# Attention A of a two-layer decoder: mask by an identity product, values and queries ahead

## The reference

```python
q_lat, c_kv, q_idx, k_idx, w_idx = split(h @ w_in)      # 16 heads of 128 latents; one c_kv of 128
c_kv = rms_norm(c_kv, latent_g)
score = sum_j w_idx[j] * relu(q_idx[j] @ k_idx.T)       # the indexer, 8 heads of 64
idx = top_k(where(causal, score, -inf), 128)            # 128 keys a query
logits = q_lat @ c_kv[idx].T * 128**-0.5 + rel_bias[bucket(t - idx)]
p = softmax(where(idx <= t, logits, -inf))
o = p @ c_kv[idx]                                       # latent, 128 wide, for each head
out = (o @ w_uv[head]) @ w_out                          # 128 -> 64 a head, 16 heads -> 1024
```

## Time and profile before

| | |
|---|---|
| runs | 1254.78, 1253.8, 1253.1 us; median 1253.8 |
| profiled execution, span from first to last instruction | 1252.3 us |
| PE busy | 1192.8 us (95%) |
| DVE busy | 638.1 us (51%) |
| ACT busy | 467.7 us (37%) |
| POOL busy | 573.3 us (46%) |
| query projection behind the indexer | 107 to 167 us |
| heads of attention A | 168 to 305 us |

### The profile page before, as it was taken

How to read it: one execution, slowest core, us unless ns; L and a number is a source line. 1 busy time by engine, 2 the same in 40 slices (tenths; PEclk the granted TensorE clock), 3 DMA queues, 4 the chain that set the end, 5 groups by cost and what they waited for, 6 DMA issues and landing times.

```text
span 1252.3 us, 16936 instructions
## 1 busy us (share of the span) xinstructions
PE 1192.8 (95%) x5580; PEld 976.2 (78%) x5580; DVE 638.1 (51%) x1095; ACT 467.7 (37%) x872; POOL 573.3 (46%) x336
## 2 busy tenths in 40 slices
PE   5999988889999999999999999899999999999996
PEld 4757877668888888888888778788888888888885
DVE  5458989995554444442222368846644444431111
ACT  4243146765333223333222367643333322232222
POOL 4333476663444444443444464304444444444441
PEclk9999999999999999999999999899999999999998
DMA  5712321102333333333333342303233333323331
GB/s 161 248 36 68 120 60 39 39 29 77 94 101 100 100 96 87 88 88 92 93 92 103 101 111 59 68 1 101 79 91 100 100 100 100 90 70 93 92 92 67
DMA packets 178709, 110.37 MB, mean 88 GB/s; under 512 B 7425, under 2 KB 173372, under 8 KB 178668
## 3 DMA queue, kind: packets, MB, share of 16 engines
q1 hardware_dynamic: 178224, 108.69, 30.4%
q10 hardware_dynamic: 444, 1.16, 0.3%
HBM read 107.70 MB, written 6.33 MB: 91 GB/s over the span
## 4 chain that ended last, share of the span: by engine, by line
PE 85%; DVE 8%; issue 3%; DMA 1%; ACT 1%; POOL 0%; DVEq 0%; ACTq 0%; SPq 0%
PE ps L608 28%; PE ps L610 27%; PE ps L609 27%; DVE prob L1547 1%; PE ps L781 1%; DVE raw L1547 1%; DMA q_all<-in_x 1%; DVE b_prob L1742 1%; DVE prob L1569 1%; DVE ss L1437 1%; DVE xs_lo L1380 1%; DVE raw L1569 1%; DVE xs_lo L1424 1%; PE ps L938 1%; DMA raw<-in_b_w_in 0%
## 5 line engine op out<-in xcount | busy, mean ns | idle before, releaser
L480 POOL TENSOR_TENSOR w_lo<-raw,w_hi 128x1024 fp32r<-128x1024 f32 (+1 forms) x200 | 462.8, 2335 | 560.2 <-ACT w_hi L1033 560.1
L608 PE MATMUL ps<-xs_hi,w_hi 128*128 128x512 f32 x960 | 380.2, 396 | 5.5 <-DVE x L1420 3.7
L609 PE MATMUL ps<-xs_lo,w_hi 128*128 128x512 f32 x960 | 374.3, 390 | 0.0
L610 PE MATMUL ps<-xs_hi,w_lo 128*128 128x512 f32 x960 | 374.2, 390 | 0.0
L1033 ACT CAST w_hi<-raw 128x1024 fp32r<-128x1024 f32 (+1 forms) x200 | 183.0, 964 | 470.2 <-PE ps L610 457.8
L608 PEld LDWEIGHTS ps<-xs_hi,w_hi 128*128 128x128 f32 x960 | 180.6, 188 | 50.9 <-issue 6.1
L610 PEld LDWEIGHTS ps<-xs_hi,w_lo 128*128 128x128 f32 x960 | 180.5, 188 | 37.9
L609 PEld LDWEIGHTS ps<-xs_lo,w_hi 128*128 128x128 f32 x960 | 180.7, 188 | 37.3 <-issue 1.2
L608 PE MATMUL ps<-act_hi,w_hi 128*128 128x512 f32 x352 | 139.2, 396 | 0.0
L610 PE MATMUL ps<-act_hi,w_lo 128*128 128x512 f32 x352 | 138.0, 392 | 0.0
L609 PE MATMUL ps<-act_lo,w_hi 128*128 128x512 f32 x352 | 136.6, 388 | 0.0
(11 more groups left out here) (191 smaller groups left out, 1568.6 us busy)
## 6 DMA issues: line engine op xcount, KB each, us to landing
raw<-in_ffn_w_gate_up SPq DMA_DIRECT2D x88, 512.0 KB, 4.9
raw<-in_ffn_w_down SPq DMA_DIRECT2D x32, 384.0 KB, 3.6
raw<-in_a_w_in SPq DMA_DIRECT2D x21, 512.0 KB, 4.6
raw<-in_ffn_w_down SPq DMA_DIRECT2D x32, 320.0 KB, 4.0
raw<-in_b_w_in SPq DMA_DIRECT2D x10, 512.0 KB, 5.1
bias_toep<-bias_row SPq DMA_DIRECT2D x1, 4096.0 KB, 19.2
toep<-bias_toep SPq DMA_DIRECT2D x16, 256.0 KB, 2.6
raw<-in_a_w_out SPq DMA_DIRECT2D x8, 512.0 KB, 4.0
```

The costliest lines, as they stand in the source:

```text
L480: nc.gpsimd.tensor_tensor(pieces(w_lo, n)[half], pieces(raw, n)[half], pieces(w_hi, n)[half].bitcast(F32), ALU.subtract)\
L608: nc.tensor.matmul(dst, wh, xh, start=start, stop=False, **kw)
L609: nc.tensor.matmul(dst, wh, xl, start=False, stop=False, **kw)
L610: return nc.tensor.matmul(dst, wl, xh, start=False, stop=stop, **kw)
```

## The change

- **Mask and bias.** POOL's sum bm is gone. PE adds the mask (written by DVE as an fp32r tile) with a product by an identity, ahead of the logits of blocks 1 to 3, and lowest adds toep straight. The causal bound of the diagonal comes in the bias table: a 33rd row of 1e30 for columns from 512 on.
- **Values ahead.** w_uv of all heads comes in one transfer; values = c @ w_uv are made once, in eight triples (values, steps 0 and 1), split by ACT and DVE into the free weight slots. The product of probabilities with them (weigh, now in step k for head k-3, two PSUM banks in turn) gives 64 columns of a head at once; the second product, o_hi, o_lo and c_hi, c_lo go.
- **Queries ahead.** q_scale writes one of two small tiles; ACT and POOL split each query during the projection into q_hi and q_lo of all 16 heads. q_scale(h) waits for q_part(h-2). Tile 15 joins the projection.
- **Slabs.** w_out's first slab is split by ACT in steps 12 and 13, its second after the last weigh; all loops over heads are written out.
- **Scaling** by 1/row sum stays on DVE, with invert at the head of the step.

The diff, cut to its core:

```diff
@@ sync @@
             slab(2, 0, wide(a_w_in[0], A_QI + 256))
+            sp.dma_start(uv_raw[:, :, :], a_w_uv[0].rearrange("h r c -> r h c")).then_inc(uv_full, 16)
             sp.wait_ge(row_out, 16)
...
-                    sp.wait_ge(bias_done, 4 * (h - 1))
+                    sp.wait_ge(neg_done, 4 * (h - 1))
@@ gpsimd @@
-            split_lo(S_A2 + 2)
-            split_lo(S_A2 + 3)
-            q_part(0, 0)
-            q_part(1, 1)
...
-                        nc.gpsimd.tensor_tensor(bm[:, OFF[i]:OFF[i] + n], toep[:, par, T - n:T], mask, ALU.add)\
-                            .then_inc(bias_done, 1)
...
+            def q_part(h):
+                if h == 0:
+                    pool.wait_ge(row_out, 16)
+                pool.wait_ge(qh_done, h + 1)
+                nc.gpsimd.tensor_tensor(q_lo[:, h, :], q_new[h % 2], q_hi[:, h, :].bitcast(F32),
+                                        ALU.subtract).then_inc(ql_done, 1)
+            for i in range(6):
+                q_part(2 * i)
+                q_part(2 * i + 1)
+                split_lo(S_A2 + 2 + i)
+                if i == 1:
+                    pool.wait_ge(uvh_done, 1)
+                    nc.gpsimd.tensor_tensor(uv_lo[:, :, :], uv_raw[:, :, :], uv_hi[:, :, :].bitcast(F32),
+                                            ALU.subtract).then_inc(uvl_done, 1)
+            for h in range(12, H):
+                q_part(h)
+            for n in range(S_AO, S_F0 + 2):
                 split_lo(n)
@@ tensor @@
-            pe.wait_ge(cn_done, 1)
-            for s in range(NB):
-                last = nc.tensor.transpose(ps[:, 7, s * P:(s + 1) * P], c_nrm[:, s * P:(s + 1) * P], ident)
-            last.then_inc(c_tr, 1)
...
             for v in range(3):
                 q_tile(v, 2)
+            tile(ps[:, 3, :], S_A2 + 7, 0, P, 256, xh, xl)
...
+            def values(j):
...
+                mm3(ps[:, 4 + s, :], cT_hi[:, s * P:(s + 1) * P], cT_lo[:, s * P:(s + 1) * P],
+                    uv_hi[:, h0:h0 + 8, :], uv_lo[:, h0:h0 + 8, :], True, True).then_inc(av_mm, 1)
+            def logits(k):
...
+                        if i:
+                            nc.tensor.matmul(ps[:, b, c0:c0 + n], ident_r[:, :], mask[:, OFF[i] - P:OFF[i] - P + n],
+                                             start=True, stop=False)
+                        last = mm3(ps[:, b, c0:c0 + n], q_hi[:, k, i * P:(i + 1) * P],
+                                   q_lo[:, k, i * P:(i + 1) * P], cT_hi[:, 0:n], cT_lo[:, 0:n], i == 0, True)
...
+            for k in range(H + 3):
+                if 2 <= k < H + 2:
+                    turn(k - 2)
+                if k >= 3:
+                    weigh(k - 3)
+                if k < H:
+                    logits(k)
+                if k < 2:
+                    for j in range(4 * k, 4 * k + 4):
+                        values(j)
...
+                if k >= H:
+                    out_first(S_AO, oT_hi, oT_lo, oTl_done, range(2 * (k - H), 2 * (k - H) + 2), 2)
@@ scalar @@
                 if i == 2:
                     split_after(S_A2)
+                    q_head(0)
+            q_head(1)
...
+            nc.scalar.copy(uv_hi[:, :, :], uv_raw[:, :, :]).then_inc(uvh_done, 1)
...
+            q_head(2)
+            for i in range(5):
+                split_after(S_A2 + 1 + i)
+                q_head(2 * i + 3)
+                q_head(2 * i + 4)
...
+            for k in range(H + 3):
+                if 2 <= k < H + 2:
+                    turned_hi(k - 2)
+                if k >= 4:
+                    heads_hi(k - 4)
+                if k < H:
+                    exponents(k)
+                if k < 2:
+                    for j in range(4 * k, 4 * k + 4):
+                        value_hi(j)
+                if k in (12, 13):
+                    split_late(S_AO, k - 12, 8)
+            heads_hi(H - 1)
+            for half in range(2):
+                split_late(S_AO + 1, half, H)
@@ vector @@
-            def q_scale(h, bank):
+            def q_scale(h, bank, par):
                 dve.wait_ge(unit_done, U_A2 + 1 + h)
-                nc.vector.scalar_tensor_tensor(q_all[:, h, :], ps[:, bank, :], -float(R) ** -0.5, rstd[:, :],
+                if not (isinstance(h, int) and h < 2):
+                    dve.wait_ge(ql_done, h - 1)
+                nc.vector.scalar_tensor_tensor(q_new[par], ps[:, bank, :], -float(R) ** -0.5, rstd[:, :],
                                                ALU.mult, ALU.mult).then_inc(qa_done, 1)
...
-            dve.wait_ge(c_h, 1)
-            lo_part(c_lo[:, :, :].rearrange("p a b -> p (a b)"), ps[:, 7, :],
-                    c_hi[:, :, :].rearrange("p a b -> p (a b)").bitcast(F32), c_l)
             for r in range(4):
                 topk_round(r)
-            q_scale(3, 3)
+            q_scale(3, 3, 1)
...
+            for k in range(H + 3):
+                if 1 <= k <= H:
+                    invert(k - 1)
+                if k >= 4:
+                    heads_lo(k - 4)
+                if 2 <= k < H + 2:
+                    turned_lo(k - 2)
+                if k < H:
+                    lowest(k)
+                if 1 <= k <= H:
+                    normalise(k - 1)
+                if k < 2:
+                    for j in range(4 * k, 4 * k + 4):
+                        value_lo(j)
+            heads_lo(H - 1)
```

More of the change, by code:

```diff
@@ new lines, in weigh @@
+            def weigh(h):
+                pe.wait_ge(ptl_done, 3 * h + 3)
+                if h >= 2:
+                    pe.wait_ge(oTl_done, h - 1)
+                for s in range(NB):
+                    c0 = (0, 4, 7, 9)[s] * P
+                    n = (NB - s) * P
+                    last = mm3(ps[:, 6 + h % 2, s * P:T], v_pair(w_hi, h, s), v_pair(w_lo, h, s),
+                               pt_hi[:, h % 2, c0:c0 + n], pt_lo[:, h % 2, c0:c0 + n], s == 0, s == NB - 1)
+                last.then_inc(o_done, 1)
@@ L849, in feed_forward @@
+            out_first(S_AO, oT_hi, oT_lo, oTl_done, range(6, DM), 2)
             def feed_forward(layer, e, s_gu, s_d):
@@ L1103, in _, with q_head @@
             split_after(2)
+            def q_head(h):
+                act.wait_ge(qa_done, h + 3)
+                nc.scalar.copy(q_hi[:, h, :], q_new[h % 2]).then_inc(qh_done, 1)
             act.wait_ge(craw_done, 1)
@@ new lines, in split_late, with turned_hi @@
+            def split_late(n, half, heads):
+                act.wait_ge(raw_full[n % 2], 32 * (n // 2 + 1))
+                act.wait_ge(o_done, heads)
+                nc.scalar.copy(pieces(w_hi, n)[half], pieces(raw, n)[half]).then_inc(hi_done, 1)
+            def turned_hi(h):
+                par = h % 2
+                for t, (b, c0, n) in enumerate(((2, 7 * P, 3 * P), (1, 4 * P, 3 * P), (0, 0, 4 * P))):
+                    act.wait_ge(pt_done, 3 * h + t + 1)
+                    if h >= 2 and t == 0:
+                        act.wait_ge(o_done, h - 1)
+                    nc.scalar.copy(pt_hi[:, par, c0:c0 + n], ps[:, 3 + b, 0:n]).then_inc(pth_done, 1)
@@ new lines, in exponents, with heads_hi @@
+            def exponents(k):
+                par = k % 2
+                for i in range(NB):
+                    at = prob[par][:, OFF[i]:OFF[i] + (i + 1) * P]
+                    act.wait_ge(neg_done, 4 * k + i + 1)
+                    nc.scalar.activation(at, at, ACT.Exp, bias=low[:, par, i:i + 1], scale=-1.0,
+                                         accum_out=rsum[:, par, i:i + 1]).then_inc(exp_done, 1)
+            def heads_hi(h):
+                act.wait_ge(o_done, h + 1)
+                nc.scalar.copy(oT_hi[own(h), h // 2, :], ps[own(h), 6 + h % 2, :]).then_inc(oTh_done, 1)
@@ L1583, in _ @@
-            for kk in range(4):
-                step(kk)
-                if kk == 1:
-                    q_scale(H - 1, 7)
-            with dve.Fori(0, 5) as i:
-                step(4, i)
-                step(5, i)
-            for kk in range(14, H + 3):
-                step(kk)
+                n = (i + 1) * P
+                nc.vector.tensor_scalar(mask[:, OFF[i] - P:OFF[i] - P + n], work[:, OFF[i] - P:OFF[i] - P + n],
+                                        TAKEN / 2, BIG, ALU.is_ge, ALU.mult).then_inc(mask_done, 1)
```

441 lines of the change are left out of this document (153 added, 288 removed).

## The result

The changed kernel takes 1266.9 us (median of four executions, 1266.1 to 1267.7) against 1253.9 us before; the ratio is 1.0101, 95% interval 1.0089 to 1.0113. That is 13.0 us slower; the forecast was 8.2 slower. 1266.9 lies in the stated range of 1255 to 1268 near its upper end, but above the forecast's own range (1258 to 1265) and in that of rival (c), 1264 to 1270. The profiled execution spans 1265.1 us, 12.8 more than before.

What follows compares the result with a forecast made beforehand. PE bounds the query projection and DVE the steady heads. Rebuilt attention -2.9, stall +8.8 and clock +2.0 give +7.9 us: span 1252.3 becomes 1260.2, median 1261.7, said as 1262; range 1255 to 1268.

Steps and rivals of the forecast that it cites:

- rival (c): Attention heads: the clock falls at step 2 or later, one to three times, 2 to 3 us each; 1264 to 1270; chance 0.20.
- clock behind it: Query tile 6, behind PE's stall: about 4 us at half clock, 2.0 us lost, bounds 0 and 3.
- P: End of the last query tile on PE; without the stall it would be 172.3 us.
- P to turn(1): Start of attention: from P to the next start of a head's last seven transposes, 18.3 us.
- thirteen periods, with the slab's split: Attention heads: 12 x 7.08 = 85.0 us, 1.2 for w_out's slab split in steps 12 and 13, one more period of 7.1.
- The queue on POOL: Query projection: q_part(3) ahead of the slab's split on POOL makes PE stand still 8.8 us at tile 6.
- the next slabs don't stall: Query projection: for later slabs POOL's chain ends some 4 us before PE gets there.
- The rings: Attention heads: chains of waits over ACT, 7.01 us, and PE, 7.08, set the period, taken as 7.1 a head.
- The marker of before: End of old attention: first out_rest product at 305.35, so 133.1 us against 130.2 for the new, saving 2.9.
- Rival (a): Attention heads: DVE's freed time counts nearly in full, period 5.5 us, 21 us less, 1241; chance 0.05.
- Rival (b): Query projection: no stall at tile 6, 1251; chance 0.05.
- (d): Heads gain a half-microsecond a period more and the stall is shorter, so they cancel: 1252 to 1256; chance 0.10.

Runs made afterwards that it cites:

- e5: Changed kernel with each slab's split ahead of its pair of queries in both POOL's and ACT's queues; 1256.7 us, ratio 1.0019.
- e1: Changed kernel with POOL splitting slab S_A2+3 ahead of q_part(2) and q_part(3); 1264.6 us, ratio 1.0079.
- e4: Changed kernel with heads_hi ahead of turned_hi on ACT and logits ahead of weigh on PE; 1245.7 us, ratio 0.9926.
- e7: Changed kernel with heads_hi ahead of turned_hi, logits ahead of weigh, and slabs ahead in POOL's (from i = 0) and ACT's queues; 1232.9 us, ratio 0.9818.
- e6: Changed kernel with the stall kept but filled by 36 extra PE products ahead of query tile 6; 1265.9 us, ratio 1.0085.
- e8: As e7, with logits(2) also ahead of turn(0) on PE; 1235.9 us, ratio 0.9849.

## Why the prediction was right, and where it was off

The sign, the place and the largest terms held. The sum by its steps, on the profiled executions:

| step | predicted | measured |
|---|---|---|
| tile 6 starts | 126.7 | 125.97 |
| PE stands still | 8.8 | 8.5 |
| clock behind it | 2.0 | 2.7 |
| P | 183.1 | 183.2 |
| P to turn(1) | 18.3 | 20.0 |
| thirteen periods, with the slab's split | 93.3 | 95.15 |
| tail to out_rest | 18.6 | 18.7 |
| out_rest before | 305.35 | 303.94 |

(For P to turn(1) and the tail, T is 0.32 us behind turn's start: 202.86 + 0.32 - 183.16 = 20.0 and 317.04 - 298.33 = 18.7.)

- **The queue on POOL.** Right in mechanism, place and size: q_scale(3) at 120.92 lies between the bounds of 120.4 and 121.9, with the hit on c_nrm. That P came out within 0.1 us is luck: the clock took 0.7 more than the 2.0 put down for it, and tile 6 started 0.7 earlier than forecast, since the whole stage began 0.6 us earlier than before (c_nrm at 105.27 against 105.88; q_scale(3), four rounds of top-k behind it, at 120.92 against 121.34 in spite of the hit). Wrong in its last paragraph ("the next slabs don't stall"): they were safe only behind the stall, and ACT's queue had the same fault. The prediction had followed POOL's alone.
- **The rings.** Right: 7.08 (PE) and 7.01 (ACT) measured 7.20 and 7.2 each alone, and 7.27 together; why the two together give 0.07 more isn't shown. The term was sized short: 93.3 against 95.15, 1.9 us. It is 0.19 us in each of thirteen periods (7.27 against 7.08), 2.4 in all, less 0.5, since the slab split in steps 12 and 13 cost 0.7 (7.66 and 7.54) and not 1.2.
- **The clock at step 2.** Off by 1.7 us: turn(0) ran at half clock behind 2.29 us of idle PE. It was rival (c), with one episode, and it came on top of the forecast; but it is a third of what the sum missed, so (c) had the number and only part of the cause. In e5's profiled execution the same idle stretch was followed by a full clock (turn(0) to turn(1) 5.27 us), and P to turn(1) is 18.4 there, as forecast. Inside that stretch two misses cancel: turn(0) comes at P+12.8 and not 13.8, and the step behind it takes 5.6 us and not 4.5. Of the traces with this idle stretch of 2.29 us, six show the fall (the changed kernel, e1 to e4, e7: turn(0) to turn(1) 6.8 to 6.9 us) and two don't (e5 and e6, 5.27 and 5.28); what decides isn't shown.
- **The marker of before.** This step was a plain misreading, worth 1.4 us. The earlier trace rows is a product of out_rest, but not the first. PE and DVE before the change, around it:

```profile
303.01 0.40 PE L610 MATMUL ps<-oT_hi,w_lo 128*128 128x512 f32 x1
...
303.94 0.40 PE L608 MATMUL ps<-oT_hi,w_hi 128*128 128x512 f32 x1
...
303.56 0.69 DVE L1600 TENSOR_TENSOR x<-ps,x 128x512 f32 x1 [1.18 <-PE ps L610]
```

The first k = 7 group of out_first ends with the product at 303.01, for DVE adds its result at 303.56; three more products finish the second group, and out_rest starts at 303.94. So from the hypothetical P of 172.3 the old attention took 131.6 us, not 133.1, and the new one was to save 1.4, not 2.9. It took 133.9. With the queues mended, P is near 171.9, out_rest starts as early as before (first addition at 303.8 against 303.56), and 344.1 against 344.7 at the last addition of out_rest. So up to the end of attention A the rest of the change measures as nothing. The 2.0 us by which e5's span is longer come later, in attention B: the clock is 0.66 in 750 to 760 and 0.56 in 810 to 820 there, against 1.00 and 0.61 before, and the additions behind it begin at 844.3 against 842.3. Whether these falls are chance or follow from the change isn't shown.
- **Behind the attention** two small things nearly cancel. From the addition that ends out_first's first group to the last one of out_rest it is 40.3 us against 41.1 before (316.7 to 357.0, 303.6 to 344.7), and up to the first addition behind attention B 0.5 us is lost (855.2 against 842.3), the clock in that stage being 0.91 (782.7 to 861.7) instead of 0.94 (771 to 850).

Sum of the misses, in the order P, P to turn(1), periods, tail, marker, out_rest, attention B: 0.1 + 1.7 + 1.9 + 0.1 + 1.4 - 0.8 + 0.5 = 4.9, and 7.9 + 4.9 = 12.8, the difference of the spans. Rival (a), that DVE's time counts nearly in full, fell in this kernel and is what e4 is: its price of 21 us was right (21.2), and its condition (heads_hi not behind turned_hi) was half of what it needs. Rival (b) fell, and (d) with it.

## What to carry to other kernels

Before crediting freed time on the busiest engine, close every ring through the new program order, and do it for each engine's queue: here two rings of equal length stood just under the old limit, and 2 us a head of freed time gave 0.3. A weight's preparation should stand in no queue behind work that depends on a slower engine, and when one such queue is mended the next slab and the next engine's queue have to be read again, since a stall hides the faults behind it. When two rings tie, remove both in one run; alone each looked like 3 to 4 us here, together they were 21. And count the clock behind an idle stretch of PE, not only the stretch: behind 2.3 us of it, six of eight traces here lost 1.6 us more.

## What the runs showed of the hardware that I had not expected

- The same 2.3 us of idle PE ahead of ten transposes was followed by a granted clock of 0.66 over 5 us in e7, and by 1.00 in e5. Joining two idle stretches of 2.3 and 1.5 us into one of 3.8 (e8) brought a fall that gave back 1.6 of the 2.3 us won.
- DVE multiplications of one SBUF tensor and a column went from 1.27 to 2.51 us for four when POOL ran sums of 2.76 us beside them, and a two-input DVE instruction from 0.75 to 1.92 beside a slab's split.
- The 128 x 512 products of out_rest come 0.229 us apart in the changed kernel (10.98 us for 48, from 335.05 to 346.03) and 0.234 before (11.24 us, from 322.20 to 333.44). Only the buffers of the moving operand differ in these lines. Why is open.
